# Differential attention: VectorE combines the first half of each tile, GpSimd the rest with a scalar form; transposes two steps behind

## Chip, cores and metric

One Trainium2 chip, one of its cores. The metric is the device time of one execution in microseconds (us): the median of three runs for the kernel before. The engines are TensorE (PE, its weight loads PEld), VectorE (DVE), ScalarE (ACT), GpSimd (POOL) and SyncE (SP), which issues most transfers.

## The reference, cut to what matters

One layer of a hybrid backbone: a projection, differential attention beside a short gated convolution, an output projection. 2048 sample tokens attend to 2048 own and 128 cached keys, with 4 heads of two score maps each; 128 prompt tokens attend to themselves. Everything is float32.

```python
s = einsum('bqhmd,bkhmd->bhmqk', qblk, k) * scale   # m = 0, 1: two maps a head
p = softmax(s, axis=-1)
a = p[:, :, 0] - lam * p[:, :, 1]
out = einsum('bhqk,bkhe->bqhe', a, v)
```

So the map a of a query tile is e0 * c0 + e1 * c1, where e0 and e1 are exponentials of the two maps and c0, c1 factors for each row (reciprocal of the row's sum, for the second map times -lam).

## The kernel before

The program has three stages: modulation, norm and input projections (to about 925 us), attention (about 930 to 1705 us), gated norm and output projection (to the end). The change touches the attention stage alone.

Attention runs over 64 tiles n = 4 * it + t, each 128 queries of one head against 2176 keys. Keys come in PIECES: columns 0 to 1023, 1024 to 2047, and the cached piece 2048 to 2175. Each engine has an order written out by hand: `step(it, t)` with four phases p, in loops over `it` with t unrolled. Phase p of a step makes the scores of map p // 2 and half p % 2 of tile n in one of two pairs of PSUM banks; the cached pieces of both maps share bank 4. Older tiles are worked on in the same step, and the constants S_COMB, S_TR, S_PV and S_OUT say by how many steps they lag.

For one tile:

- TensorE (`scores`, L761) makes the scores; VectorE takes the negated maximum of each 1024 columns (L1380) and of the cached pieces (L1411); ScalarE takes the exponential into e0 (four buffers) and e1 (two buffers) in SBUF, with row sums (L1070, cached pieces L1057). The scores of phase p + 2 need the banks that the exponential of phase p reads.
- VectorE brings the pieces' maxima together (L1402, L1405), ScalarE takes factors (L1082), and in phase 0 of the next step VectorE makes sums and reciprocals (L1388, L1394, L1398).
- GpSimd (`factors`) waits for the reciprocals, makes the row factors (L596, L598), scales the three pieces of e1 (L603) and the middle piece of e0 (L606) and adds the middle piece (L610). Scaling is a tensor_tensor product with the factor repeated along the row.
- VectorE (`combine`, L1362) does the first and the cached piece in one instruction each, two steps later: e0 * c0 + scaled e1. The first stands in phase 0, between the first maximum and the copy of transposes; the cached one in phase 2, before the cached pieces' maxima.
- TensorE (`transposes`, L742) turns the 17 blocks of the map around, three steps behind, in groups of 4, 4, 4, 4 and 1. ScalarE copies groups 0, 1, 2 and 4 to `at` (L1023), VectorE group 3 (`tr_dve`, L1355). Groups 1 and 3 share a bank, so group 1 of the next tile waits for VectorE's copy (t_dve).
- TensorE (`product`, L750) multiplies pairs of tiles with the values, half of the key blocks in each step; ScalarE evacuates (`att_out`, L1031) and stores (`att_store`).

SyncE loads the queries of the next `it` tile by tile behind the scores (L389), the keys of the next head, and the values of a new head in two parts (`load_v`, L402) once the last product on the old ones is done. After tile 63 the steps drain; the prompt's attention and the first output weights are worked in between (`prompt_maps`, `wo_lo`, L1347).

VectorE's phase 0 before, as the order in its queue:

```python
reduce max p0; combine(n - 2, first piece); L1388; tr_dve(n - 4); L1394; L1398
```

Of the kernel before, what the change touches and what calls it, by code (L numbers as in the profile page):

```python
# [26 lines left out]
ALU = mybir.AluOpType  # L27
# [3 lines left out]
P = 128  # L31
# [30 lines left out]
S_COMB, S_TR, S_PV, S_OUT = 2, 3, 5, 7  # L62
# [12 lines left out]
def hymba_layer(nc, a):  # L75
# [8 lines left out]
    with ctx:  # L84
# [25 lines left out]
        tick = sb("tick", [P, 1])  # L110
        cw = sb("cw", [P, 4])
# [199 lines left out]
        def _(sp):  # L311
# [157 lines left out]
            for it in range(ITS):  # L469
                head = it // 4  # L470
                for t in range(4):
# [6 lines left out]
                    if it % 4 == 0 and head > 0 and t == 3:  # L478
                        sp.wait_ge(pv_mm, 4 * it - 1)
                        load_v(head, 0)  # L480
                    if it % 4 == 1 and head > 0 and t == 0:
                        sp.wait_ge(pv_mm, 4 * (it - 1))
                        load_v(head, 1)
# [62 lines left out]
        def _(pool):  # L546
# [46 lines left out]
            def factors(n, t):  # L593
# [7 lines left out]
                for c in (0, 2, 1):  # L601
                    k0, k1 = PIECES[c]
                    pool.tensor_tensor(e1[:, b, k0:k1], e1[:, b, k0:k1],  # L603
                                       stt[:, b, 7, 3 + c:4 + c].to_broadcast([P, k1 - k0]), ALU.mult)\
                        .then_inc(e1_done, 1)
                pool.tensor_tensor(e0[:, t, k0:k1], e0[:, t, k0:k1], stt[:, b, 7, 1:2].to_broadcast([P, k1 - k0]), ALU.mult)\  # L606
                    .then_inc(e0_done, 1)
                pool.wait_ge(e1_done, 3 * (n + 1))
                pool.wait_ge(e0_done, n + 1)
                pool.tensor_tensor(e0[:, t, k0:k1], e0[:, t, k0:k1], e1[:, b, k0:k1], ALU.add).then_inc(a1_ready, 1)  # L610
# [9 lines left out]
        def _(pe):  # L620
# [109 lines left out]
            def transposes(n, t, g):  # L730

                j0, cnt = TGROUPS[g]
                if g == 0:
                    pe.wait_ge(a_ready, 2 * (n + 1))
                    pe.wait_ge(a1_ready, n + 1)
# [28 lines left out]
            def step(it, t, sc=True, tr=True, tr_last=True, pv=True):  # L764
                n = 4 * it + t
                for p in range(4):
# [12 lines left out]
                    if pv:  # L779
                        half = 1 - t % 2  # L780
                        b = 0 if t in (1, 2) else 1
                        if p == 1 - half:
                            pe.wait_ge(s_v[half], (32 if half else 16) * ((it + (2 if t == 0 else 3)) // 4))
                            if half == 0:
                                pe.wait_ge(t_act, 4 * (n - 4) + 3)
                                wait(pe, att_evac, 2 * it - (2 if t == 1 else 1))
                            else:
                                pe.wait_ge(t_act, 4 * (n - 4))
                                pe.wait_ge(t_dve, n - 4)
# [18 lines left out]
            for n in range(NT, NT + S_PV):  # L808
# [3 lines left out]
                if n == NT + 4:  # L812
# [42 lines left out]
        def _(act):  # L855
# [170 lines left out]
            def att_out(it, t):  # L1026

                pb = 1 if t == 1 else 0
                act.wait_ge(pv_mm, 4 * it + t - S_PV)
                wait(act, att_stored[pb], 16 * (it - (2 if t == 1 else 1)))  # L1030
                act.activation(atto[:, pb], ps[:, 7, pb * 2 * P:(pb + 1) * 2 * P], ACT.Copy).then_inc(att_evac, 1)  # L1031

            def att_store(it, t):

                pb = 1 if t == 1 else 0
                act.wait_ge(att_evac, 2 * it - (2 if t == 1 else 1))
                u = it - (2 if t == 1 else 1)
# [7 lines left out]
            def step(it, t, sc=True, tr=True, tr_last=True, out=True):  # L1045
                n = 4 * it + t
                b = t % 2
                for p in range(4):
# [3 lines left out]
                    if sc and p == 3:  # L1052
                        act.wait_ge(mxc_done, n + 1)
                        wait(act, a_ready, 2 * (n - 1))
# [6 lines left out]
                    if sc:  # L1061
# [3 lines left out]
                        if p == 2:  # L1065
                            wait(act, a_ready, 2 * (n - 1) - 1)
                        if p == 3:
                            wait(act, a1_ready, n - 1)
# [15 lines left out]
            for it in range(3):  # L1084
                for t in range(4):
                    n = 4 * it + t
                    step(it, t, tr=n >= S_TR, tr_last=n > S_TR, out=n >= S_OUT and t % 2 == 1)
            with act.Fori(3, ITS) as it:
                for t in range(4):
                    step(it, t, out=t % 2 == 1)  # L1090
            for n in range(NT, NT + S_OUT - 1):
                step(n // 4, n % 4, sc=False, tr=n < NT + S_TR, tr_last=n <= NT + S_TR,
                     out=n % 2 == 1)
# [4 lines left out]
                if n == NT + 2:  # L1098
                    act.wait_ge(a_ready, 2 * NT)
# [46 lines left out]
        def _(dve):  # L1146
# [211 lines left out]
            def combine(n, t, c):  # L1358

                k0, k1 = PIECES[c]  # L1360
                dve.wait_ge(e1_done, 3 * n + (1 if c == 0 else 2))
                dve.scalar_tensor_tensor(e0[:, t, k0:k1], e0[:, t, k0:k1], stt[:, t % 2, 7, c:c + 1],  # L1362
# [8 lines left out]
            def step(it, t, sc=True, den=True, comb=True, tr_last=True):  # L1371
                n = 4 * it + t
                b = t % 2
                for p in range(4):
# [9 lines left out]
                    if p == 0 and comb:  # L1384
                        combine(n - S_COMB, (t - S_COMB) % 4, 0)
# [4 lines left out]
                    if p == 0 and tr_last:  # L1390
# [168 lines left out]
```

## Time and profile before

| | us |
|---|---|
| median of 3 runs (1937.11 to 1943.31) | 1938.04 |
| the profiled execution | 1940.76 |
| its span | 1939.0 |
| TensorE busy | 1763.6 |
| VectorE busy | 1173.9 |
| ScalarE busy | 720.2 |
| GpSimd busy | 749.1 |

The mean granted TensorE clock is 0.971 of full speed. Busy times are sums over the whole span; a matmul's end is modelled, so TensorE's busy time is not work at peak. In lists of groups, a line shows the engine, the operation, output and input, shapes, count, busy time and the mean of one, and behind the bar the idle time in front of it with what ended it. In a timeline, columns are start and length in us; the bracket gives the idle time of the engine just before and its releaser.

### The profile page before, as it was taken

The numbers are of one execution on the slowest core, as the hardware profiler recorded it, in microseconds if no ns is written. First come the engines' busy times: TensorE is split into PE (matmuls) and PEld (weight loads), VectorE is DVE, ScalarE is ACT, GpSimd is POOL, SyncE is SP. The second block draws the span as 40 slices with busy tenths as digits, with TensorE's granted clock in tenths as the row PEclk, the third lists the DMA queues.
The fourth block names the chain that finished last, engine by engine and source line by source line (L and its number), as shares of the span: only waits on it lengthen the run. The fifth ranks groups of instructions, "written<-read, shape, count | busy, mean of one in ns | idle before, by whom it ended". The sixth has DMA issues, their size and how long they took to land.

```text
span 1939.0 us, 25390 instructions
## 1 busy us (share of the span) xinstructions
PE 1763.6 (91%) x8596; PEld 1488.4 (77%) x8596; DVE 1173.9 (61%) x1500; ACT 720.2 (37%) x1505; POOL 749.1 (39%) x614
## 2 busy tenths in 40 slices
PE   7799999989999999998589999889999999659999
PEld 2478888878999989998367777767777777548889
DVE  0554588872232332423688888888888888655553
ACT  2443233331010100100466666666666666431110
POOL 0000488880000000000477777777777777400000
PEclk9899999999999999999799999999999999879999
DMA  9233222331020110101710031113001100146441
GB/s 352 95 109 104 80 99 91 105 117 52 29 90 19 41 68 28 68 19 45 186 35 29 27 85 39 31 47 79 27 27 51 53 27 16 46 170 241 176 141 48
DMA packets 121890, 154.79 MB, mean 80 GB/s; under 512 B 10224, under 2 KB 111344, under 8 KB 120688
## 3 DMA queue, kind: packets, MB, share of 16 engines
q1 hardware_dynamic: 116704, 149.69, 24.0%
q10 hardware_dynamic: 5136, 4.46, 0.7%
q8 instruction: 28, 0.46, 0.1%
q14 instruction: 22, 0.18, 0.0%
HBM read 104.04 MB, written 50.07 MB: 79 GB/s over the span
## 4 chain that ended last, share of the span: by engine, by line
PE 68%; DVE 16%; issue 6%; DMA 4%; ACT 3%; SPq 2%; POOL 0%; DVEq 0%; ACTq 0%; POOLq 0%
PE ps L634 34%; PE ps L836 10%; PE ps L761 8%; DVE e L1362 8%; PE ps L750 7%; PE ps L742 4%; PE ps L626 3%; DVE stt L1380 2%; ACT scr L919 2%; PE ps L651 2%; DVE at L1355 1%; DMA wad<-in_w_ada 1%; PE ps L819 1%; DMA worw<-in_w_out 1%; ACT scr L881 1%
## 5 line engine op out<-in xcount | busy, mean ns | idle before, releaser
L634 PE MATMUL ps<-hT,w 128*128 128x448 f32 (+1 forms) x3360 | 694.1, 366 | 12.6 <-DVE w L1169 12.6
L634 PEld LDWEIGHTS ps<-hT,w 128*128 128x128 f32 x3360 | 623.9, 189 | 76.2 <-issue 27.1
L761 PE MATMUL ps<-kb,qb 128*128 (+1 forms) x1280 | 340.0, 397 | 47.9 <-ACT e L1070 30.8
L1070 ACT ACTIVATE e<-ps,stt 128x1024 f32<-128x1024 f32 x256 | 285.7, 1116 | 259.3 <-DVE stt L1380 235.7
L1380 DVE TENSOR_REDUCE stt<-ps 128x1 f32<-128x1024 f32 x256 | 312.2, 1220 | 97.3 <-PE ps L761 96.9
L750 PE MATMUL ps<-at,vb 128*128 128x256 f32 x1088 | 281.2, 390 | 9.2 <-ACT atto L1031 9.2
L761 PEld LDWEIGHTS ps<-kb,qb 128*128 128x128 f32 x1280 | 208.1, 194 | 84.3 <-ACT e L1070 39.3
L596 POOL TENSOR_TENSOR stt<-stt,lamc 128x2 f32<-128x2 f32 x64 | 12.6, 197 | 660.9 <-DVE stt L1398 660.9
L603 POOL TENSOR_TENSOR e<-e,stt 128x1024 f32<-128x1024 f32 (+1 forms) x192 | 262.8, 1397 | 5.0
L750 PEld LDWEIGHTS ps<-at,vb 128*128 128x128 f32 x1088 | 211.1, 197 | 48.4 <-issue 9.7
L742 PE MATMUL ps<-cst,e 128*128 128x128 f32 x1088 | 175.7, 280 | 57.6 <-DVE at L1355 56.6
L1362 DVE SCALAR_TENSOR_TENSOR e<-e,stt 128x1024 f32<-128x1024 f32 (+1 forms) x128 | 225.6, 1762 | 0.0
L742 PEld LDWEIGHTS ps<-cst,e 128*128 128x128 f32 x1088 | 131.0, 142 | 112.0 <-DVE at L1355 82.1
L836 PE MATMUL ps<-mix,wo 128*128 128x448 f32 (+1 forms) x960 | 205.1, 373 | 7.2 <-DVE mix L1455 7.2
L836 PEld LDWEIGHTS ps<-mix,wo 128*128 128x128 f32 x960 | 181.7, 192 | 27.5 <-DVE mix L1455 7.6
L610 POOL TENSOR_TENSOR e<-e 128x1024 f32<-128x1024 f32 x64 | 152.5, 2383 | 9.2
L985 ACT ACTIVATE scr<-ps 128x448 f32<-128x448 f32 (+1 forms) x40 | 20.9, 533 | 352.7 <-PE ps L634 352.7
L1217 DVE RECIPROCAL qx<-qx 128x448 f32<-128x448 f32 (+1 forms) x40 | 114.8, 2870 | 49.8 <-ACT qx L950 49.7
L565 POOL TENSOR_TENSOR qx<-qx,scr 128x448 f32<-128x448 f32 (+1 forms) x40 | 45.8, 1146 | 241.3 <-DVE qx L1221 238.9
L1023 ACT ACTIVATE at<-ps 128x512 f32<-128x512 f32 (+1 forms) x256 | 124.3, 511 | 23.1 <-PE ps L742 22.8
L606 POOL TENSOR_TENSOR e<-e,stt 128x1024 f32<-128x1024 f32 x64 | 125.2, 1956 | 0.0
L634 PE MATMUL ps<-w,hT 128*128 128x512 f32 x408 | 98.1, 401 | 7.3 <-DVE hT L1201 7.3
(108 smaller groups left out, 1374.4 us busy)
## 6 DMA issues: line engine op xcount, KB each, us to landing
raw<-in_w_in SPq DMA_DIRECT2D x32, 512.0 KB, 3.8
qb<-spill_q SPq DMA_DIRECT2D x256, 64.0 KB, 2.3
wad<-in_w_ada SPq DMA_DIRECT2D x6, 2048.0 KB, 9.0
scr<-in_xT SPq DMA_DIRECT2D x8, 1024.0 KB, 5.7
kb<-spill_k SPq DMA_DIRECT2D x8, 1024.0 KB, 9.7
spill_k<-scr SPq DMA_DIRECT2D x32, 224.0 KB, 2.1
spill_q<-scr SPq DMA_DIRECT2D x32, 224.0 KB, 2.2
spill_cv<-scr SPq DMA_DIRECT2D x32, 224.0 KB, 2.2
```

What stands on the lines that cost most here:

```text
L603: pool.tensor_tensor(e1[:, b, k0:k1], e1[:, b, k0:k1], stt[:, b, 7, 3 + c:4 + c].to_broadcast([P, k1 - k0]), ALU.mult)\
L606: pool.tensor_tensor(e0[:, t, k0:k1], e0[:, t, k0:k1], stt[:, b, 7, 1:2].to_broadcast([P, k1 - k0]), ALU.mult)\
L610: pool.tensor_tensor(e0[:, t, k0:k1], e0[:, t, k0:k1], e1[:, b, k0:k1], ALU.add).then_inc(a1_ready, 1)
L634: mm = pe.matmul(out, slot_of(l, j), rhs_of(r, j), start=(i == 0 and j == 0), stop=(i == 2 and j == DJ - 1))
L742: mm = pe.transpose(trbank(g)[:, i * P:(i + 1) * P], e0[:, t, (j0 + i) * P:(j0 + i + 1) * P], ident)
L750: mm = pe.matmul(ps[:, 7, b * 2 * P:(b + 1) * 2 * P], vb[:, js[i]], at[:, b, 0, js[i], :], start=(half == 0 and i == 0), stop=(half == 1 a ...
L761: mm = pe.matmul(out[:, c0 - k0:c1 - k0], qb[:, t, ver, m], keys, start=(ver == 0), stop=(ver == 1))
L836: mm = pe.matmul(ps[:, k % 4, 0:n], wo[:, o, l, j], mix[:, tg % 2, r, j, 0:n], start=(half == 0 and i == 0 and j == H), stop=(half == 1 an ...
L1023: act.activation(at[:, t // 2, 0, j0:j0 + cnt, (t % 2) * P:(t % 2 + 1) * P], trbank(g).rearrange("p (j q) -> p j q", j=cnt), ACT.Copy).the ...
L1070: act.activation(dst[:, c * 1024:(c + 1) * 1024], ps[:, 2 * c:2 * c + 2, :].rearrange("p c n -> p (c n)"), ACT.Exp, bias=stt[:, b, 0, 3 * ...
L1362: dve.scalar_tensor_tensor(e0[:, t, k0:k1], e0[:, t, k0:k1], stt[:, t % 2, 7, c:c + 1], e1[:, t % 2, k0:k1], ALU.mult, ALU.add).then_inc(a ...
L1380: dve.tensor_reduce(stt[:, b, 0, 3 * m + c:3 * m + c + 1], ps[:, 2 * c:2 * c + 2, :].rearrange("p c n -> p (c n)"), AX.X, ALU.max, negate= ...
```

## The change

- VectorE keeps one combine a tile, of the first piece. It is issued one step behind the scores (two before), in phase 2 behind the cached pieces' maxima. The copy of transposes moves to directly behind the first maximum.
- GpSimd scales e1 in the order of its pieces and both later pieces of e0, with tensor_scalar and a factor for each partition in place of tensor_tensor, and adds both pieces in one instruction of 1152 columns. A small product into a new tile `gate` stands ahead of the scaling.
- Transposes lag by two steps (three before), products by four (five), the evacuation by six (seven). Group 0 waits for VectorE's combine alone, group 2 for GpSimd's add. All waits on counters, the parity of halves and buffers, and the places of the value loads are moved to match. The drain has one step less.

```diff
-S_COMB, S_TR, S_PV, S_OUT = 2, 3, 5, 7
+S_COMB, S_TR, S_PV, S_OUT = 1, 2, 4, 6
...
+        gate = sb("gate", [P, 2])
...
-                    if it % 4 == 0 and head > 0 and t == 3:
+                    if it % 4 == 0 and head > 0 and t == 2:
...
-                    if it % 4 == 1 and head > 0 and t == 0:
-                        sp.wait_ge(pv_mm, 4 * (it - 1))
+                    if it % 4 == 0 and head > 0 and t == 3:
+                        sp.wait_ge(pv_mm, 4 * it)
...
-                for c in (0, 2, 1):
+                pool.tensor_tensor(gate[:], lamc[:], lamc[:], ALU.mult)
+                for c in range(3):
...
-                    pool.tensor_tensor(e1[:, b, k0:k1], e1[:, b, k0:k1],
-                                       stt[:, b, 7, 3 + c:4 + c].to_broadcast([P, k1 - k0]), ALU.mult)\
+                    pool.tensor_scalar(e1[:, b, k0:k1], e1[:, b, k0:k1], stt[:, b, 7, 3 + c:4 + c], None, ALU.mult)\
...
-                pool.tensor_tensor(e0[:, t, k0:k1], e0[:, t, k0:k1], stt[:, b, 7, 1:2].to_broadcast([P, k1 - k0]), ALU.mult)\
-                    .then_inc(e0_done, 1)
+                for c in (1, 2):
+                    k0, k1 = PIECES[c]
+                    pool.tensor_scalar(e0[:, t, k0:k1], e0[:, t, k0:k1], stt[:, b, 7, c:c + 1], None, ALU.mult)\
+                        .then_inc(e0_done, 1)
...
-                pool.wait_ge(e0_done, n + 1)
-                pool.tensor_tensor(e0[:, t, k0:k1], e0[:, t, k0:k1], e1[:, b, k0:k1], ALU.add).then_inc(a1_ready, 1)
+                pool.wait_ge(e0_done, 2 * (n + 1))
+                pool.tensor_tensor(e0[:, t, 1024:KEYS], e0[:, t, 1024:KEYS], e1[:, b, 1024:KEYS], ALU.add)\
+                    .then_inc(a1_ready, 1)
...
-                    pe.wait_ge(a_ready, 2 * (n + 1))
+                    pe.wait_ge(a_ready, n + 1)
+                if g == 2:
                    pe.wait_ge(a1_ready, n + 1)
...
-                        half = 1 - t % 2
-                        b = 0 if t in (1, 2) else 1
+                        half = t % 2
+                        b = t // 2
...
-                            pe.wait_ge(s_v[half], (32 if half else 16) * ((it + (2 if t == 0 else 3)) // 4))
+                            pe.wait_ge(s_v[half], (32 if half else 16) * ((it + 3) // 4))
...
-                                pe.wait_ge(t_act, 4 * (n - 4) + 3)
-                                wait(pe, att_evac, 2 * it - (2 if t == 1 else 1))
+                                pe.wait_ge(t_act, 4 * (n - 3) + 3)
+                                wait(pe, att_evac, 2 * it - (2 if t == 0 else 1))
...
-                                pe.wait_ge(t_act, 4 * (n - 4))
-                                pe.wait_ge(t_dve, n - 4)
+                                pe.wait_ge(t_act, 4 * (n - 3))
+                                pe.wait_ge(t_dve, n - 3)
...
-                if n == NT + 4:
+                if n == NT + 3:
...
             def att_out(it, t):
...
-                pb = 1 if t == 1 else 0
+                pb = 1 if t == 0 else 0
...
-                wait(act, att_stored[pb], 16 * (it - (2 if t == 1 else 1)))
+                wait(act, att_stored[pb], 16 * (it - (2 if t == 0 else 1)))
...
             def att_store(it, t):
...
-                pb = 1 if t == 1 else 0
-                act.wait_ge(att_evac, 2 * it - (2 if t == 1 else 1))
-                u = it - (2 if t == 1 else 1)
+                pb = 1 if t == 0 else 0
+                act.wait_ge(att_evac, 2 * it - (2 if t == 0 else 1))
+                u = it - (2 if t == 0 else 1)
...
-                        wait(act, a_ready, 2 * (n - 1))
+                        wait(act, a1_ready, n - 1)
...
-                            wait(act, a_ready, 2 * (n - 1) - 1)
-                        if p == 3:
-                            wait(act, a1_ready, n - 1)
+                            wait(act, a_ready, n - 1)
...
-                    step(it, t, tr=n >= S_TR, tr_last=n > S_TR, out=n >= S_OUT and t % 2 == 1)
+                    step(it, t, tr=n >= S_TR, tr_last=n > S_TR, out=n >= S_OUT and t % 2 == 0)
...
-                    step(it, t, out=t % 2 == 1)
+                    step(it, t, out=t % 2 == 0)
...
-                     out=n % 2 == 1)
+                     out=n % 2 == 0)
...
-                    act.wait_ge(a_ready, 2 * NT)
+                    act.wait_ge(a_ready, NT)
...
-            def combine(n, t, c):
...
-                k0, k1 = PIECES[c]
-                dve.wait_ge(e1_done, 3 * n + (1 if c == 0 else 2))
-                dve.scalar_tensor_tensor(e0[:, t, k0:k1], e0[:, t, k0:k1], stt[:, t % 2, 7, c:c + 1],
+            def combine(n, t):
...
+                k0, k1 = PIECES[0]
+                dve.wait_ge(e1_done, 3 * n + 1)
+                dve.scalar_tensor_tensor(e0[:, t, k0:k1], e0[:, t, k0:k1], stt[:, t % 2, 7, 0:1],
...
             def bc(x):
...
-                    if p == 0 and comb:
-                        combine(n - S_COMB, (t - S_COMB) % 4, 0)
+                    if p == 0 and tr_last:
+                        tr_dve(n - 1 - S_TR, (t - 1 - S_TR) % 4)
...
-                    if p == 0 and tr_last:
-                        tr_dve(n - 1 - S_TR, (t - 1 - S_TR) % 4)
...
-                    if p == 2 and comb:
-                        combine(n - S_COMB, (t - S_COMB) % 4, 2)
...
+                    if p == 2 and comb:
+                        combine(n - S_COMB, (t - S_COMB) % 4)
...
-            for n in range(NT, NT + S_TR + 1):
+            for n in range(NT, NT + S_TR + 2):
...
```

## Rows read from the trace of the kernel before

**Rows 1.** The page, part 1: busy time, share of the span and instructions of each engine.

```profile
PE 1763.6 (91%) x8596; PEld 1488.4 (77%) x8596; DVE 1173.9 (61%) x1500; ACT 720.2 (37%) x1505; POOL 749.1 (39%) x614
```

**Rows 2.** Busy time by windows in the attention stage: stretch, its length, engines, granted clock, DMA.

```profile
982.00:1660.00 678.00, 607.64 (x3167) 492.60 (x3168) 578.53 (x764) 441.00 (x1027) 515.42 (x413) 0.98 0.15 40
```

**Rows 3.** Waits from 982 to 1660 us: total, times, longest.

```profile
ACT e L1070 <- DVE stt L1380: 188.4, 219, 2.5
POOL stt L596 <- DVE stt L1398: 145.0, 59, 4.1
...
PE ps L742 <- DVE at L1355: 50.8, 30, 1.7
...
PE ps L761 <- ACT e L1070: 19.2, 30, 0.8
```

**Rows 4.** Timeline of one tile and of the context maximum two tiles on.

```profile
1187.83 0.41 DVE L1411 TENSOR_REDUCE stt<-ps 128x2 f32<-128x256 f32 x1
...
1189.41 1.11 ACT L1070 ACTIVATE e<-ps,stt 128x1024 f32<-128x1024 f32 x1 [0.32 <-DVE stt L1380]
...
1189.81 2.38 POOL L610 TENSOR_TENSOR e<-e 128x1024 f32<-128x1024 f32 x1
1189.85 1.22 DVE L1380 TENSOR_REDUCE stt<-ps 128x1 f32<-128x1024 f32 x1
...
1190.66 1.20 PE L761 MATMUL ps<-kb,qb 128*128 x4 [0.69 <-ACT e L1070]
1190.99 2.27 DVE L1362 SCALAR_TENSOR_TENSOR e<-e,stt 128x1024 f32<-128x1024 f32 x1
1191.19 1.11 ACT L1070 ACTIVATE e<-ps,stt 128x1024 f32<-128x1024 f32 x1 [0.21 <-DVE stt L1380]
...
1193.26 0.68 DVE L1355 COPY at<-ps 128x512 f32<-128x512 f32 x1
...
1194.00 0.66 PE L742 MATMUL ps<-cst,e 128*128 128x128 f32 x4 [1.70 <-DVE at L1355]
...
1194.29 0.20 POOL L596 TENSOR_TENSOR stt<-stt,lamc 128x2 f32<-128x2 f32 x1 [2.10 <-DVE stt L1398]
...
1194.84 4.10 POOL L603 TENSOR_TENSOR e<-e,stt 128x1024 f32<-128x1024 f32 x3
...
1198.90 1.94 POOL L606 TENSOR_TENSOR e<-e,stt 128x1024 f32<-128x1024 f32 x1
...
1210.52 0.41 DVE L1411 TENSOR_REDUCE stt<-ps 128x2 f32<-128x256 f32 x1
```

**Rows 5.** Groups by shape, 930 to 1690 us.

```profile
L1380 DVE TENSOR_REDUCE stt<-ps 128x1 f32<-128x1024 f32 x256 | 312.2, 1220 | 97.3 <-PE ps L761 96.9
...
L1362 DVE SCALAR_TENSOR_TENSOR e<-e,stt 128x1024 f32<-128x1024 f32 x64 | 116.2, 1815 | 0.0
...
L1362 DVE SCALAR_TENSOR_TENSOR e<-e,stt 128x128 f32<-128x128 f32 x64 | 109.4, 1709 | 0.0
```

**Rows 6.** Timeline of the drain.

```profile
1666.14 0.33 DVE L1362 SCALAR_TENSOR_TENSOR e<-e,stt 128x128 f32<-128x128 f32 x1
...
1670.95 2.87 POOL L606 TENSOR_TENSOR e<-e,stt 128x1024 f32<-128x1024 f32 x1
...
1681.98 1.28 DVE L1362 SCALAR_TENSOR_TENSOR e<-e,stt 128x1024 f32<-128x1024 f32 x1
...
1683.91 1.11 PE L742 MATMUL ps<-cst,e 128*128 128x128 f32 x4 [3.92 <-DVE at L1355]
```

**Rows 7.** Timeline of TensorE's weight loads, a quarter of a step: its first and its end.

```profile
1185.87 0.76 PEld L761 LDWEIGHTS ps<-kb,qb 128*128 128x128 f32 x4
...
1188.10 0.77 PEld L761 LDWEIGHTS ps<-kb,qb 128*128 128x128 f32 x4
```

**Rows 8.** Timeline near the start of attention: L1405.

```profile
947.19 1.30 DVE L1405 TENSOR_TENSOR stt<-stt 128x6 f32<-128x6 f32 x1
```

**Rows 9.** DMA issues: count, KB each, median us from issue to landing.

```profile
vb<-spill_v SPq DMA_DIRECT2D x4, 576.0 KB, 4.0
```

## Prediction

> **What bounds the kernel now.** The page's busy shares come first [rows 1]: TensorE 91%, no other engine above 61%. That is a mean over stages; the change lies only in the attention stage, 64 query tiles from about 930 to 1700 us, so I read that one. The windows [rows 2] give for 982 to 1660 us TensorE 607.6 of 678 us, 90%, so 70 us of idle time in 59 tiles (GpSimd waits for reciprocals 59 times, once a tile [rows 3]), 1.2 us each. VectorE is busy 578.5 and GpSimd 515.4 us there: both are close behind. The waits [rows 3] name what TensorE's idle time ends with: 50.8 us on VectorE's copy of transposes (L1355), 19.2 us on ScalarE's exponential (L1070). The exponential itself waits for VectorE's maxima (188.4 us).
>
> The timeline of one tile [rows 4] shows why. GpSimd's add starts at 1189.81 and lasts 2.38 us. VectorE starts its 1024-column combine at 1190.99; it lasts 2.27 us and ends 1.07 us behind the end of the add. Behind it in VectorE's queue stands the copy (1193.26), and TensorE's next transposes start at 1194.00 after 1.70 us of idle time. The 128-column combine is worse by its size: 1709 ns on average [rows 5], 0.33 us when GpSimd is idle [rows 6]. So a VectorE instruction with two inputs in SBUF stands still until GpSimd's current instruction ends. It works the other way too: beside VectorE's L1347, GpSimd's L606 takes 2.87 us at 1670.95 [rows 6] in place of 1.94 at 1198.90 [rows 4].
>
> A tile takes (1210.52 - 1187.83) / 2 = 11.35 us by the context maxima of tiles two apart [rows 4]; over the 678 us it is 11.49, since the granted clock is 0.98 of 2.4 GHz on average there [rows 2]. I take that as unchanged.
>
> **The parts and their cost, for a tile.**
> *TensorE: nothing added.* A quarter of a step (4 score matmuls, 4 product instructions, 4 transposes) runs from 1185.87 to 1188.10, 2.23 us [rows 7]. Four are 8.9; the context scores (4 shorter matmuls, which I estimate at half of the quarter's 4 long ones, 0.45), the 17th transpose (0.14) and the odd product instruction (0.21) make 9.7 to 9.9 us. I take 9.85: the floor, 1.5 us below today.
>
> *VectorE.* It loses the 128-column combine (0.33 us of work, 1.71 with its wait), keeps the 1024-column one (1.28 us when alone [rows 6], 1815 ns on average [rows 5]), and the copy now stands directly behind the first maximum. Work: 4 maxima of 1.22, context 0.41, combine 1.28, copy 0.68 and five small ones of some 0.16, 8.0 us. That is under the floor; only its waits count. The wait of the transposes for the copy falls from 1.70 us to about 0.2 in even tiles: first maximum 1.2 us after its scores, copy done 1.8 later, the transposes due at 2.8.
>
> *GpSimd.* Small operations 0.55 us (1194.29 to 1194.84 [rows 4]) and one more, the gate, some 0.27: 0.82. Scaling grows from 3200 columns to 2176 + 1152 = 3328. The add grows to 1152 columns, 2.38 x 1.125, with its gap 2.8. The combine holds GpSimd up once, 1.1. At today's price for scaling, 4.10 for 2176 columns [rows 4] and 1.94 + 0.3 for 1152, the total is 0.82 + 6.35 + 2.8 + 1.1 = 11.1 us. **The unknown is the price of the scalar form**, which no row shows. Upper end: the same as L603, (4.10 - 0.3) / 2 = 1.90 for 1024 columns. Lower end: 1.22, the price of the one-stream maximum on VectorE (L1380) [rows 5]; another engine, so a far row. Two full streams cost 2.38 (L610) [rows 4] and one stream with a repeated scalar 1.90; I take the same step of 0.48 once more, 1.42. That saves 3.25 x 0.48 = 1.56: a loop of 9.5 us. To it comes up to 0.6 us (from VectorE's small operations to GpSimd's first) where GpSimd has to wait for the reciprocals: 10.1. At the lower end it is 8.9.
> The Trainium skill, GPSIMD Engine Reference, section Engine selection, says that one-input operations on GpSimd run at about line rate and two-input ones about twice as slowly. By it the scaling would be near my lower end, and the sum the one of the first rival; no run here shows it yet.
>
> *The combine's new place.* It stands between the context maxima and the last maximum, and GpSimd is in mid-stream there. VectorE's next instruction starts some 0.08 us before the end of the one ahead (1189.85 + 1.22 against 1190.99) [rows 4], so the maximum takes 1.14, the context 0.33, the combine 1.20, and the last maximum starts 2.66 us behind the third, where TensorE spaces the scores by 2.23: 0.4 late. The wait for the end of a scaling is half of 1.42 on average, 0.7. From the last maximum to the scores of the next tile that need its bank it is 2.6 us (maximum to exponential 1.34, 1189.85 to 1191.19; exponential to score 1.25, 1189.41 to 1190.66), and 1.2 from the last scores to an undelayed maximum: 3.8 together. TensorE gets there 3.8 us behind the last scores where little product work lies between, every second tile, and 5.5 in the others. So every second tile loses all of 0.4 + 0.7 = 1.1, the others nothing: 0.55 per tile. With 0.1 for the copy and 0.1 for L1405, another two-input instruction (1.30 us when it met GpSimd [rows 8], one of the small ones otherwise), the tile takes 9.85 + 0.75 = 10.6 us.
>
> *Transposes two steps behind.* ScalarE's first exponential no longer waits for the last transposes of the same step; what that gives is inside the 1.5 us already. The transposes of tile n need the combine of the step before, ready 1.5 us early, and GpSimd's add only for their third group, some 4 us early. Behind that new wait stand the third transposes and the last scores; if GpSimd is later than that, it is the bound, below. The value loads get fewer steps: each issue waits for the last product on the old values, and lands 4.0 us later [rows 9], with more than a step (10 us) until its first product; the query load queued behind it on SP is for the next iteration, 40 us away. Cost 0. The buffers' waits in ScalarE (second tensor of exponentials) now name work finished a step earlier: 0.
>
> *Drain.* After the last tile VectorE works off the prompt's maps before the copy that TensorE waits for (3.92 us, 1683.91 [rows 6]), unchanged. Behind it lies one step less: some 3.7 us of product and 2.4 of transposes, part of which an output-weight load may eat. I take 5 (0 to 7).
>
> **Sum.** 11.35 - 10.6 = 0.75 x 62 steady tiles = 46.5, plus 5: 51.5 us off. The profiled execution took 1940.8 us (span 1939.0), 2.7 above the median of 1938.0. 1940.8 - 51.5 - 2.7 = **1886.5 us**. Own range: 10.4 to 10.8 us a tile, 1874 to 1901.
>
> **Rivals.**
> *TensorE becomes the bound.* The scalar form costs 1.2 or less, GpSimd is done early and VectorE meets it rarely: 10.1 to 10.3 us, 1.15 x 62 = 71 + 6: 1861. For it: the one-input form. Against: three two-input VectorE instructions per tile still meet GpSimd.
> *The port takes it back.* The combine or L1405 falls into the 2.7 us add instead of a 1.4 us scaling. Every second tile then loses 2.7 rather than 1.1, and the next maximum is late too: about 11.1 us, 0.25 x 62 + 4 = 20 off: 1918. For it: L1362 waits in both its forms today [rows 5], and the add is GpSimd's longest instruction. Against: where the combine sits, a scaling is due, not the add. The Trainium skill, SBUF — State Buffer, section Who interferes with whom, states the block as a rule: a VectorE instruction with two SBUF inputs against a GpSimd one that reads SBUF, and the second to come stands still until the other ends. By that rule, which the trace bears out, moving the combine into mid-stream speaks against the change.
> *GpSimd becomes the bound, slower than before.* The scalar form costs what L603 costs. The loop is 11.1 with reciprocals ready in time (16 off, and up to 5 in the drain: 1917 to 1922; nearer to no change with some of the latency), and 11.7 where the add ends first and reciprocals come after it: +0.35 x 62 - 5 = +17: 1955 from the median of 1938. It decides from a scaling price of about 1.8 us per 1024 columns, where the loop with its latency passes 11.35. For it: the loop scales 4% more columns and adds 12.5% more. Against: an operand less.
> *The change does nothing*: waits only change names; 1938.
>
> **Chances.** Forecast 0.42; TensorE bound 0.18; port 0.15; GpSimd bound without the latency 0.08 (0.05 of it faster by more than 0.3%); nothing 0.05; slower 0.12. 0.3% is 5.8 us, about what a measurement can tell here. Faster 0.42 + 0.18 + 0.15 + 0.05 = 0.80, the same 0.08, slower 0.12. The range goes from the TensorE bound (1856) to just short of no change (1936): below lies little, above the slower case and part of no change.
>
> **What would show it.** Right: GpSimd's TENSOR_SCALAR near 1.4 us, the context maxima 10.6 us apart, TensorE's wait for L1355 nearly gone, its wait for L1070 up, combine about 1.9 us on average, VectorE's idle time larger. Wrong: scalings at 1.9 us and GpSimd's idle time before L596 (145.0 us now [rows 3]) gone; or combines over 3 us beside the add; or a new TensorE wait for GpSimd's add before the third group of transposes.

## The result, and the profile after

The changed kernel takes 2032.2 us (median of 4, 2030.65 to 2033.11) against 1937.6 before: ratio 1.048, 95% interval 1.046 to 1.050. It is slower by 94.6 us, where 51.5 us less were forecast, outside the stated range. Experiment 6 below had one slow execution, of 3503 us; its time is given as 1906.0 us, the median of its other three, where the recorded expectations name 1906.9, the median of all four.

The groups of the attention stage in the profile after (by shape, 930 to 1790 us) name the cause in their first line:

```profile
L605 POOL TENSOR_SCALAR e<-e,stt 128x1024 f32<-128x1024 f32 x128 | 362.6, 2845 | 0.1
...
L609 POOL TENSOR_SCALAR e<-e,stt 128x1024 f32<-128x1024 f32 x64 | 182.0, 2844 | 0.0
L613 POOL TENSOR_TENSOR e<-e 128x1152 f32<-128x1152 f32 x64 | 169.3, 2646 | 5.6
...
L1365 DVE SCALAR_TENSOR_TENSOR e<-e,stt 128x1024 f32<-128x1024 f32 x64 | 136.4, 2131 | 136.7 <-POOL e L605 136.7
...
L605 POOL TENSOR_SCALAR e<-e,stt 128x128 f32<-128x128 f32 x64 | 40.0, 625 | 0.0
```

Before, the same view (930 to 1690 us) had these two lines for e1:

```profile
L603 POOL TENSOR_TENSOR e<-e,stt 128x1024 f32<-128x1024 f32 x128 | 242.5, 1895 | 5.0
...
L603 POOL TENSOR_TENSOR e<-e,stt 128x128 f32<-128x128 f32 x64 | 25.7, 402 | 0.0
```

A scaling of 1024 columns in the scalar form takes 2.845 us, where the tensor_tensor form with a repeated factor took 1.895. The operation with fewer operands is half as dear again. VectorE was idle for 136.7 us in front of its combine (L1365), waiting for the first scaling of e1 (L605).

The timeline of GpSimd over one tile after, with what stands beside it (start, length):

```profile
1188.37 0.20 POOL L597 TENSOR_TENSOR stt<-stt,lamc 128x2 f32<-128x2 f32 x1
...
1189.09 6.25 POOL L605 TENSOR_SCALAR e<-e,stt 128x1024 f32<-128x1024 f32 x3
...
1191.97 2.13 DVE L1365 SCALAR_TENSOR_TENSOR e<-e,stt 128x1024 f32<-128x1024 f32 x1 [1.69 <-POOL e L605]
...
1195.32 3.42 POOL L609 TENSOR_SCALAR e<-e,stt 128x1024 f32<-128x1024 f32 x2
...
1195.54 0.90 DVE L1406 TENSOR_TENSOR stt<-stt 128x6 f32<-128x6 f32 x1
...
1198.83 2.65 POOL L613 TENSOR_TENSOR e<-e 128x1152 f32<-128x1152 f32 x1
...
1201.43 0.19 POOL L597 TENSOR_TENSOR stt<-stt,lamc 128x2 f32<-128x2 f32 x1
...
1207.22 0.66 PE L747 MATMUL ps<-cst,e 128*128 128x128 f32 x4 [1.69 <-DVE e L1365]
```

L597 opens each tile's work on GpSimd, and none of its rows here has idle time in front of it: from 1188.37 to 1201.43 it works without a gap, 13.06 us. Before, L596 had waited 2.10 us there [rows 4]. The loop is 0.72 of small operations, 6.23 for e1, 3.51 for e0 and 2.60 for the add. The other engines wait for it in turn, TensorE at L747 through the combine. The windows from 982 to 1740 us say the same: GpSimd busy 744 of 758 us, TensorE 646 (85%, before 90% [rows 2]), and a granted clock of 0.91:

```profile
982.00:1740.00 758.00, 646.12 (x3138) 523.58 (x3137) 533.68 (x697) 436.15 (x1016) 744.01 (x523) 0.91 0.14 36
```

A tile took 11.52 us before and takes 13.06 now (means over 40 tiles, between the 6th and the 46th context maximum from 980 us on; all tile times below are made so). 1.54 x 62 = 95 us: the loss lies in the tiles. The stall that the change was to remove did go: TensorE's wait for the copy, 50.8 us before [rows 3], is no longer among its larger waits after. A wait of the same size, for the combine, has taken its place (982 to 1740 us):

```profile
PE ps L766 <- ACT e L1073: 58.5, 47, 1.7
PE ps L747 <- DVE e L1365: 50.8, 29, 1.9
```

### The profile page after: what moved, and what is told of

It is laid out like the page before. It is cut to its first block, busy times and chain, and to the rows that moved or that the text cites. A ratio compares the mean times of both kernels' runs of the same rounds, so it can differ in the third digit from the quotient of the medians.

```text
span 2028.9 us, 25262 instructions
## 1 busy us (share of the span) xinstructions
PE 1809.1 (89%) x8596; PEld 1528.5 (75%) x8596; DVE 1133.4 (56%) x1436; ACT 720.6 (36%) x1505; POOL 1007.0 (50%) x742
## 4 chain that ended last, share of the span: by engine, by line
PE 47%; POOL 31%; issue 12%; DVE 4%; DMA 3%; ACT 3%; SPq 0%; POOLq 0%; ACTq 0%; DVEq 0%
PE ps L638 33%; POOL e L605 19%; PE ps L841 9%; POOL e L613 6%; POOL e L609 3%; PE ps L630 3%; ACT scr L924 2%; PE ps L655 1%; DMA wad<-in_w_ada 1%; PE ps L824 1%; POOL stt L599 1%; DMA worw<-in_w_out 1%; POOL gate L602 1%; ACT scr L886 1%; DVE crs L1444 1%
## 5 line engine op out<-in xcount | busy, mean ns | idle before, releaser
L766 PE MATMUL ps<-kb,qb 128*128 (+1 forms) x1280 | 371.0, 426 | 87.2 <-ACT e L1073 68.7
L605 POOL TENSOR_SCALAR e<-e,stt 128x1024 f32<-128x1024 f32 (+1 forms) x192 | 401.1, 2105 | 0.1
L766 PEld LDWEIGHTS ps<-kb,qb 128*128 128x128 f32 x1280 | 231.2, 216 | 134.8 <-issue 54.9
L755 PE MATMUL ps<-at,vb 128*128 128x256 f32 x1088 | 285.9, 394 | 0.0
L597 POOL TENSOR_TENSOR stt<-stt,lamc 128x2 f32<-128x2 f32 x64 | 12.6, 196 | 504.9 <-DVE stt L1399 504.9
L747 PE MATMUL ps<-cst,e 128*128 128x128 f32 x1088 | 188.7, 293 | 63.8 <-DVE e L1365 54.4
L747 PEld LDWEIGHTS ps<-cst,e 128*128 128x128 f32 x1088 | 143.8, 151 | 115.8 <-issue 36.2
L609 POOL TENSOR_SCALAR e<-e,stt 128x1024 f32<-128x1024 f32 (+1 forms) x128 | 219.2, 1725 | 0.0
L1365 DVE SCALAR_TENSOR_TENSOR e<-e,stt 128x1024 f32<-128x1024 f32 x64 | 136.4, 2131 | 136.7 <-POOL e L605 136.7
L613 POOL TENSOR_TENSOR e<-e 128x1152 f32<-128x1152 f32 x64 | 169.3, 2646 | 5.6
```

The costliest lines, as they stand in the source:

```text
L605: pool.tensor_scalar(e1[:, b, k0:k1], e1[:, b, k0:k1], stt[:, b, 7, 3 + c:4 + c], None, ALU.mult)\
L609: pool.tensor_scalar(e0[:, t, k0:k1], e0[:, t, k0:k1], stt[:, b, 7, c:c + 1], None, ALU.mult)\
L613: pool.tensor_tensor(e0[:, t, 1024:KEYS], e0[:, t, 1024:KEYS], e1[:, b, 1024:KEYS], ALU.add)\
L747: mm = pe.transpose(trbank(g)[:, i * P:(i + 1) * P], e0[:, t, (j0 + i) * P:(j0 + i + 1) * P], ident)
L755: mm = pe.matmul(ps[:, 7, b * 2 * P:(b + 1) * 2 * P], vb[:, js[i]], at[:, b, 0, js[i], :], start=(half == 0 and i == 0), stop=(half == 1 a ...
L766: mm = pe.matmul(out[:, c0 - k0:c1 - k0], qb[:, t, ver, m], keys, start=(ver == 0), stop=(ver == 1))
```

## The experiments

Each is timed against the kernel before on the same chip. The chips are four: experiments 1 to 3 ran on one, 5 to 8 on another, 9 to 11 on a third, 12 and 13 on a fourth, and the kernel before took 1938.5, 1940.7, 1938.7 and 1938.5 us on them. Differences of a few us between experiments of different chips are therefore uncertain by some 2 us.

| | us | ratio to before, 95% | us per tile |
|---|---|---|---|
| 1 changed, tensor_tensor form | 1917.3 | 0.988 (0.984 to 0.991) | 11.22 |
| 2 before, scalar form | 2022.6 | 1.042 (1.039 to 1.045) | 13.03 |
| 3 changed, constant factor (one execution) | 2004.1 | | 12.62 |
| 4 changed, scaling and add in one instruction | no result | | |
| 5 as 1, no gate | 1906.4 | 0.983 (0.981 to 0.985) | 11.08 |
| 6 as 5, one scaling on ScalarE | 1906.0 | 0.981 (0.979 to 0.983) | 11.08 |
| 7 changed, one scaling on ScalarE | 1893.1 | 0.976 (0.975 to 0.978) | 10.85 |
| 8 as 1, lags of before | 1923.7 | 0.992 (0.990 to 0.993) | 11.22 |
| 9 as 6, factors' differences on ScalarE | 1860.8 | 0.960 (0.958 to 0.962) | 10.29 |
| 10 as 7, the same | 1864.9 | 0.960 (0.958 to 0.963) | 10.30 |
| 11 as 5, the same | 1906.2 | 0.983 (0.981 to 0.986) | 11.08 |
| 12 before, with both additions of 9 | 1891.1 | 0.976 (0.973 to 0.979) | 10.74 |
| 13 changed, differences on ScalarE | 2033.6 | 1.049 (1.046 to 1.052) | 13.07 |

**1. The changed kernel with the old form.**

```diff
-pool.tensor_scalar(e1[:, b, k0:k1], e1[:, b, k0:k1], stt[:, b, 7, 3 + c:4 + c], None, ALU.mult)
+pool.tensor_tensor(e1[:, b, k0:k1], e1[:, b, k0:k1], stt[:, b, 7, 3 + c:4 + c].to_broadcast([P, k1 - k0]), ALU.mult)
...
-pool.tensor_scalar(e0[:, t, k0:k1], e0[:, t, k0:k1], stt[:, b, 7, c:c + 1], None, ALU.mult)
+pool.tensor_tensor(e0[:, t, k0:k1], e0[:, t, k0:k1], stt[:, b, 7, c:c + 1].to_broadcast([P, k1 - k0]), ALU.mult)
```

> The changed kernel, with GpSimd's five scalings back in the tensor_tensor form with a repeated factor (columns, order, gate, lags and all waits as changed). Theory P (price of the scalar form): scalings fall from 2.84 to 1.9 us per 1024 columns, GpSimd's loop from 13.06 to 10.1 us plus up to 1.1 for VectorE's combine; a tile takes 10.8 to 11.3 us and the kernel 1890 to 1920 us, faster than before. Theory S (the schedule: the combine in mid-stream on VectorE and the shorter lag of the transposes cost the time): it stays above 1980 us whatever the scalings cost.

Measured: 1917.3 us. Theory P holds: 115 us lie in the form alone, and the rest of the change, the gate included, is worth 21 us of gain. The timeline of this kernel:

```profile
1179.06 5.08 POOL L605 TENSOR_TENSOR e<-e,stt 128x1024 f32<-128x1024 f32 x3
...
1180.99 2.90 DVE L1365 SCALAR_TENSOR_TENSOR e<-e,stt 128x1024 f32<-128x1024 f32 x1
...
1185.32 0.69 DVE L1406 TENSOR_TENSOR stt<-stt 128x6 f32<-128x6 f32 x1
...
1187.67 1.43 DVE L1391 TENSOR_TENSOR stt<-stt 128x6 f32<-128x6 f32 x1
...
1189.58 0.20 POOL L597 TENSOR_TENSOR stt<-stt,lamc 128x2 f32<-128x2 f32 x1 [0.49 <-DVE stt L1399]
...
1200.80 0.20 POOL L597 TENSOR_TENSOR stt<-stt,lamc 128x2 f32<-128x2 f32 x1 [0.49 <-DVE stt L1399]
```

The combine starts at 1180.99, just behind the start of the second scaling, and ends at 1183.89: it takes 1.6 us longer than alone (1.28 us [rows 6]) and then holds GpSimd up itself (the three scalings of e1 take 5.08 here, 4.10 before [rows 4]). The three two-input instructions of VectorE (L1365, L1406, L1391) take 5.0 us in a tile, against 1.28 + 0.17 + 0.15 alone: 3.4 us of waiting. GpSimd idles 0.49 us for the reciprocals.

**2. The kernel before with the new form**, and the gate.

```diff
+pool.tensor_tensor(gate[:], lamc[:], lamc[:], ALU.mult)
-pool.tensor_tensor(e1[:, b, k0:k1], e1[:, b, k0:k1], stt[:, b, 7, 3 + c:4 + c].to_broadcast([P, k1 - k0]), ALU.mult)
+pool.tensor_scalar(e1[:, b, k0:k1], e1[:, b, k0:k1], stt[:, b, 7, 3 + c:4 + c], None, ALU.mult)
...
-pool.tensor_tensor(e0[:, t, k0:k1], e0[:, t, k0:k1], stt[:, b, 7, 1:2].to_broadcast([P, k1 - k0]), ALU.mult)
+pool.tensor_scalar(e0[:, t, k0:k1], e0[:, t, k0:k1], stt[:, b, 7, 1:2], None, ALU.mult)
```

> The kernel before, with its scalings on GpSimd in the tensor_scalar form and the gate ahead of them, nothing else. Theory P: GpSimd's loop is 0.8 of small ones + 2 x 2.84 + 0.6 + 2.84 + 0.1 + 2.4 = 12.4 us and becomes the bound, with the latency of the reciprocals up to 13.0; the kernel takes 2000 to 2045 us, so that the form alone makes it as slow as the whole change. Theory S: GpSimd's waiting time of 2.5 us per tile hides most of it and it stays within 1940 to 1965 us.

Measured: 2022.6 us, 13.03 us a tile. The form, with the gate, costs 84 us in the old schedule. With the first experiment it brackets the cause from both sides. The gate stands in this kernel and in the changed one; from start to start it takes 0.28 us, so that its part where GpSimd has no gap is 0.28 x 62 = 17 us by an estimate. No run takes it out of a kernel with the scalar form.

**3. A constant in place of the factor.** The row factors are left out of the scaled pieces here.

```diff
-pool.tensor_scalar(e1[:, b, k0:k1], e1[:, b, k0:k1], stt[:, b, 7, 3 + c:4 + c], None, ALU.mult)
+pool.tensor_scalar(e1[:, b, k0:k1], e1[:, b, k0:k1], 0.25, None, ALU.mult)
...
-pool.tensor_scalar(e0[:, t, k0:k1], e0[:, t, k0:k1], stt[:, b, 7, c:c + 1], None, ALU.mult)
+pool.tensor_scalar(e0[:, t, k0:k1], e0[:, t, k0:k1], 0.25, None, ALU.mult)
```

> The changed kernel, with the constant 0.25 in place of the factor read from SBUF in all five scalings (the row factors are left out of the scaled pieces, so the maps lack their reciprocals there). If reading the factor per partition is what makes the form slow, a scaling of 1024 columns falls well below 1.9 us and the kernel below 1930. If the form itself is slow, it stays at 2.84 us and the kernel at 2032.

The groups of this kernel:

```profile
L605 POOL TENSOR_SCALAR e<-e 128x1024 f32<-128x1024 f32 x128 | 352.4, 2771 | 0.0
...
L605 POOL TENSOR_SCALAR e<-e 128x128 f32<-128x128 f32 x64 | 34.2, 535 | 0.0
```

Measured: 2004.1 us in one execution, 12.62 us a tile. Reading the factor costs 0.07 us, the form 2.77. It is the form. The kernel is 28 us faster than the 2032 expected, since each of the five scalings is 0.07 to 0.09 us shorter: 0.4 us a tile. The difference between 1024 and 128 columns is 2.24 us for 896, 2.5 ns a column, so it is a cost of each column and not of starting. For the tensor_tensor form the same working gives (1895 - 402) / 896 = 1.7 ns a column.

**4. GpSimd's scaling and add of e0 in one instruction** (scalar_tensor_tensor), with e1 scaled in the tensor_tensor form. It was expected to take 1860 to 1890 us if the fused form cost what the add does, and 1880 to 1920 us if forms with a factor for each partition are slow as a family. There is no result, so the price of that form on GpSimd, and whether such forms are slow as a family, stay open.

**5. Without the gate.** One instruction of 0.19 us (0.28 from start to start) less on GpSimd.

```diff
-pool.tensor_tensor(gate[:], lamc[:], lamc[:], ALU.mult)
```

> The first experiment (tensor_tensor form in the changed schedule) without the small gate operation. There GpSimd's loop is 11.22 us and nearly closed (L597 at 1189.58 and 1200.80), so theory P, in which that loop sets the tile, wants 0.27 us less per tile: 10.9 to 11.0 us and 1897 to 1908 us. If VectorE's chain (busy 640 of 658 us, waits included) or TensorE sets the pace, the gate is hidden and the time stays at 1917.

Measured: 1906.4 us; a tile 0.14 shorter, so that 11.08 us is just above the 10.9 to 11.0 expected. Some 9 to 11 us for one tiny instruction: GpSimd's loop is on the path also with the cheap form, but about half of what is taken from it comes back in waits. The change's schedule alone, with the old form and no gate, is worth 34 us of gain (1906.4 against 1940.7 on that chip).

**6. One scaling moved to ScalarE** (tensor_tensor form). GpSimd scales e1's cached piece first here, then the middle one.

```diff
+if fac and p == 1:
+    act.wait_ge(coef_done, n)
+    act.activation(e1[:, 1 - b, 0:1024], e1[:, 1 - b, 0:1024], ACT.Copy, scale=stt[:, 1 - b, 7, 3:4]).then_inc(sc_done, 1)
...
-for c in range(3):
+for c in (2, 1):
...
-dve.wait_ge(e1_done, 3 * n + 1)
+dve.wait_ge(sc_done, n + 1)
```

> The changed schedule with the tensor_tensor form and no gate, and the scaling of e1's first piece moved from GpSimd to ScalarE (one copy of 1024 columns with a factor per partition, in phase 1). GpSimd's loop loses 1.9 us: 11.0 - 1.9 = 9.1. Theory P: GpSimd is off the critical path, TensorE's 9.85 us and the waits of the maxima are left, a tile takes 10.1 to 10.6 us and the kernel 1845 to 1885 us. If meeting GpSimd at the port is the dearer part, VectorE's waits keep the tile at 10.8 or more, above 1895 us.

Measured: 1906.0 us, 11.08 us a tile: the same as without the move. Theory P missed; its rival, a tile of 10.8 us or more and over 1895 us, came true. GpSimd now waits 2.30 us before L598, in the first line (982 to 1660 us), so it is not the bound. The timeline shows what is:

```profile
POOL stt L598 <- DVE stt L1403: 136.8, 60, 2.3
```

```profile
1191.51 2.63 POOL L613 TENSOR_TENSOR e<-e 128x1152 f32<-128x1152 f32 x1
...
1192.35 0.16 DVE L1407 TENSOR_REDUCE stt<-stt 128x2 f32<-128x6 f32 x1
...
1192.55 1.61 DVE L1410 TENSOR_TENSOR stt<-stt 128x6 f32<-128x6 f32 x1
...
1194.08 1.21 DVE L1387 TENSOR_REDUCE stt<-ps 128x1 f32<-128x1024 f32 x1
1194.19 0.21 ACT L1089 ACTIVATE stt<-stt 128x6 f32<-128x6 f32 x1 [0.71 <-DVE stt L1410]
```

A subtraction of 6 columns takes 1.61 us in place of 0.17: it has two inputs in SBUF, arrives in the middle of the add and ends with it (1194.16 against 1194.14). The reduction just ahead of it (L1407), with one input in SBUF, takes 0.16 us beside the same add. The next tile's first maximum and ScalarE's factors stand behind the subtraction. This is the rival of the prediction in which L1405 is caught by the add.

**7. The same move with the slow form kept** (gate too).

> The same move to ScalarE, with GpSimd's other four scalings kept in the changed kernel's tensor_scalar form and the gate kept. GpSimd's loop is 13.06 - 2.84 = 10.2 us. Theory P: the tile takes 10.2 to 10.8 us and the kernel 1855 to 1900 us, though the form is slow. VectorE's combine meets the scalar form for 0.85 us (2.13 against 1.28) where it stood 1.6 us beside the other form (2.87), so it may come close to the version with the tensor_tensor form. If the scalar form harms in another way than by its length, it stays above 1930 us.

Measured: 1893.1 us, 12.9 less than with the fast form. The expectation held for the kernel's time, and its second half more than I had thought; the tile, 10.85 us, is just above the 10.2 to 10.8. The groups of this kernel:

```profile
L610 POOL TENSOR_SCALAR e<-e,stt 128x1024 f32<-128x1024 f32 x64 | 204.7, 3198 | 0.0
...
L614 POOL TENSOR_TENSOR e<-e 128x1152 f32<-128x1152 f32 x64 | 169.6, 2649 | 9.5
...
L1370 DVE SCALAR_TENSOR_TENSOR e<-e,stt 128x1024 f32<-128x1024 f32 x64 | 98.7, 1542 | 47.6 <-ACT e L1086 47.6
...
L1411 DVE TENSOR_TENSOR stt<-stt 128x6 f32<-128x6 f32 x64 | 19.0, 297 | 2.2
```

and of the sixth, VectorE's two:

```profile
L1369 DVE SCALAR_TENSOR_TENSOR e<-e,stt 128x1024 f32<-128x1024 f32 x64 | 120.2, 1879 | 13.5 <-ACT e L1085 10.8
L1410 DVE TENSOR_TENSOR stt<-stt 128x6 f32<-128x6 f32 x64 | 102.4, 1600 | 2.2
```

Here the combine takes 1.54 us on average and the subtraction 0.30, against 1.88 and 1.60 in the sixth. GpSimd is fuller, but VectorE waits less at it.

**8. The lags of the kernel before**, in the first experiment's kernel.

```diff
-S_COMB, S_TR, S_PV, S_OUT = 1, 2, 4, 6
+S_COMB, S_TR, S_PV, S_OUT = 1, 3, 5, 7
```

with the parities, counters and load places of before.

> The first experiment with the lags of the kernel before: transposes three steps behind, products five, the evacuation seven, with their parities and load places; the new split of the work and VectorE's new order are kept. Theory P: the shorter lag is worth only the drain, so 1917 plus 3 to 8 us. Theory S would have the shorter lag cost time in every tile: then it is faster than 1917 by 10 us or more.

Measured: 1923.7 us with the same 11.22 us a tile. Transposes two steps behind are worth some 4 to 6 us: 6.4 between the two medians, 4.2 when each is set against the kernel before on its own chip. They lie in the drain: from the last context maximum to the end of the program it is 281.5 us here and 275.9 in experiment 1.

**9 to 11. The subtraction taken from VectorE**, in the sixth, seventh and fifth kernels. ScalarE forms the differences inside the exponentials, two of 0.29 us in place of one of 0.21.

```diff
-act.wait_ge(d_done, n + 1)
-act.activation(stt[:, b, 3, :], stt[:, b, 2, :], ACT.Exp).then_inc(f_done, 1)
+act.wait_ge(gm_done, n + 1)
+for m in range(2):
+    fm = act.activation(stt[:, b, 3, 3 * m:3 * m + 3], stt[:, b, 0, 3 * m:3 * m + 3], ACT.Exp,
+                        scale=-1.0, bias=stt[:, b, 5, 2 + m:3 + m])
+fm.then_inc(f_done, 1)
...
-dve.tensor_tensor(three(stt[:, b, 2, :]), bc(stt[:, b, 5, 2:4]), three(stt[:, b, 0, :]), ALU.subtract)
```

> The sixth experiment (tensor_tensor form, e1's first piece scaled on ScalarE; 1906.9 us, a tile 11.07 us) with VectorE's small two-input subtraction taken away: ScalarE takes the differences inside its two exponentials of the factors. Theory Q (the port holds the tile: the subtraction stands 1.43 us behind GpSimd's 2.6-us add in every tile, and the factors, the next maximum and the copy stand behind it): a tile loses 0.5 to 1.0 us, 10.1 to 10.6 us, the kernel 1845 to 1880. Rival R (ScalarE, 76% busy there, or TensorE sets the pace): at most 10 us off, above 1895.

> The seventh experiment (tensor_scalar form, e1's first piece on ScalarE; 1893.1 us) with the same subtraction taken away. There it waited only 0.13 us on average (297 ns for one), and the product L1396 waits 0.83 us behind the add instead. Theory Q: 0 to 0.3 us per tile, 1875 to 1893, a far smaller gain than in its neighbour, since the wait it removes is small. Rival R: the same small change in both.

> The fifth experiment (tensor_tensor form, no gate, all scalings on GpSimd; 1906.4 us, a tile 11.09 us) with the same subtraction taken away. GpSimd's loop there is closed but for 0.5 us (10.6 busy with the combine's hold-up). Theory P: GpSimd stays the bound, so the removal of a VectorE wait gives at most 0.5 us per tile, 1875 to 1906. If VectorE's chain set the tile instead, it would gain the 0.5 us of wait and more, below 1870.

The ninth took 1860.8 us and 10.29 us a tile, inside theory Q's ranges: some 45 us from one instruction of 6 columns, 0.79 us in each tile. The windows of it, 982 to 1600 us:

```profile
982.00:1600.00 618.00, 595.41 (x3247) 500.80 (x3245) 475.90 (x655) 511.45 (x1160) 508.97 (x420) 1.00 0.17 46
```

TensorE is busy 96% here: it is the bound at last. The tenth gained 28.2 us, more than the 0 to 18 expected, a miss: the VectorE product ahead of the reciprocals (L1396 in the seventh, L1399 here) falls from 984 to 303 ns on average too, so moving one instruction took the next one out of the add's way. The eleventh gained nothing (1906.2): all scalings are on GpSimd there, its loop of 11.08 us is closed but for 0.5, and the wait saved at the subtraction reappears at the product (1884 ns on average). So the same edit is worth 45, 28 or 0 us, depending on who sets the tile.

**12. Both additions without the change.**

> The kernel before (its schedule, split and lags) with the two additions of the ninth experiment: ScalarE scales e1's first piece and takes the factors' differences. GpSimd's loop shrinks to 7.2 us, which it had 2.5 us to spare for anyway; VectorE's combines still stand ahead of the copy, but the add ahead of them ends about 1.9 us earlier. If the additions alone make the ninth fast, this comes within 10 us of 1861. If the changed kernel's order on VectorE and its lags carry part of it, as I hold, this lands at 1880 to 1930 us.

Measured: 1891.1 us, within the band for the changed kernel's schedule carrying a part. The additions alone bring 47 us, and the change's own schedule 30.3 on top of them, the ninth's time being 1860.8. The other order of counting agrees: the schedule first is worth 34 us (experiment 5) and the additions then some 44 to 46. The schedule is the new split of the work, VectorE's order and the lags together; only the lags were tried by themselves (experiment 8).

**13. The changed kernel without the subtraction's wait.**

> The changed kernel with the factors' differences on ScalarE and nothing else: the 0.73-us wait of VectorE's subtraction in every tile goes, GpSimd's loop of 13.06 us stays. Theory P: GpSimd alone sets the tile, so the kernel stays within 5 us of 2032. If VectorE's waits at the port are part of what made the change slow, it gains 0.3 to 0.7 us per tile, 1985 to 2012.

Measured: 2033.6 us, no change. VectorE's waits at the port cost nothing in the changed kernel, since GpSimd alone sets its tile.

## Why the prediction was wrong, step by step

- **The price of the scalar form: the step that failed.** "Upper end: the same as L603" took for granted that an operand less can't cost more, and the chosen 1.42 carried a trend on from two rows. It measured 2.84. In the loop this term is 3.25 x 1.42 = 4.6 us larger than taken. The prediction's loop of 9.5 us becomes 14.1 by it; 13.06 was measured (0.72 + 9.74 for the five scalings + 2.60), since the hold-up of 1.1 in that sum did not occur. Experiments 1 and 2 put 115 and 84 us on the form, the second with the gate. By the Trainium skill, GPSIMD Engine Reference, section Engine selection, one-input operations run at about line rate and two-input ones about twice as slowly; for this form the runs say the opposite (2.84 us for one input, 2.38 for the add with two [rows 4]), and the measurement decides.
- **GpSimd becomes the bound.** The mechanism was among the rivals, with 0.12 where slower, but its price ended at L603's, so 1955 was the worst that it gave. It would have decided "from a scaling price of about 1.8 us". At 1.89 (experiment 1) the kernel was still faster: the loop came to 10.73 of work and hold-up plus 0.49 for the reciprocals, 11.22, near the 11.1 given and under the 11.7 that I feared. The 1917 to 1922 stated for that case met 1917.3, in part by luck: the loop's work was 0.4 us less than the 11.1 taken with reciprocals in time, and the wait for them gave it back. The sign of being wrong came as stated, but for the price: GpSimd's idle time before its first instruction of a tile (145.0 us before [rows 3]) is gone.
- **The combine's new place.** The hold-up of GpSimd, taken as 1.1, measured 0.97 with the old form (the 128-column scaling behind the combine takes 1.38 in place of 0.41) and 0 with the new. Its wait, taken as 0.7 on average, was 1.6 with the old form and 0.85 with the new. The 0.7 took the meeting for one at a random moment of a scaling. It is not random: the combine needs e1's first piece, so it can't start before the first scaling ends. In the timelines it starts 0.06 us (changed kernel) and 0.08 us (experiment 1) behind the start of the second scaling, and meets that one from its beginning.
- **L1405 at 0.1 us: mis-sized.** It waits 0.73 us in the changed kernel and 1.43 in experiment 6, where it sets the tile; taking it away gave 45 us. The port rival had the mechanism right.
- **The copy.** Right: the wait of 50.8 us went. The new wait of 50.8 us for the combine is GpSimd's lateness.
- **TensorE's floor.** 9.85 us was the estimate, and 10.1 to 10.3 the tile with TensorE as the bound, 1861 us. Experiment 9 reached 10.29 us and 1860.8 with TensorE 96% busy, which is 9.9 us a tile and agrees with the floor. It is another kernel than the rival's, so that the same microsecond is luck.
- **The tile before.** The sum starts from 11.35 us, one pair of tiles; the mean is 11.52. From there to the 10.6 forecast it would have been 57 us and not 46.5. It doesn't bear on the direction.
- **The lags and the drain.** Taken as 5 us, measured 4 to 6 (experiment 8); nothing in a tile, as said. In the changed kernel the gain doesn't show: from the last context maximum to the end it is 278.6 us, and 279.1 before.
- **SP's loads: 0.** No wait for values or queries is among the larger ones after.

## What to carry to other kernels

An operation whose price no row shows has no upper end in the row of a richer operation: on GpSimd the form with fewer operands was the dearer one here (2.84 us against 1.90). Run the one instruction before a schedule is built on it. An engine with 2 us to spare in 11 turned into the bound when three long scalings on it changed their form (experiment 2), and what is won elsewhere is then invisible (experiment 13). A tiny VectorE instruction with two inputs in SBUF can cost what is left of a long GpSimd one that it meets (1.43 us for 6 columns); on ScalarE the same work made one exponential of 0.21 us into two of 0.29.

## What the runs showed that I had not expected

GpSimd's two forms keep VectorE waiting in different ways. In the old form a scaling holds a two-input VectorE instruction off until it ends: the combine takes 2.90 us at 1180.99. In the changed kernel the combine at 1191.97 stands beside this scaling, the second of the merged row of L605:

```profile
1191.92 2.85 POOL L605 TENSOR_SCALAR e<-e,stt 128x1024 f32<-128x1024 f32 x1
```

It starts 0.06 us behind it and takes 2.13, so that it ends 0.7 us ahead of that scaling's end, and the subtraction at 1195.54 ends 1.12 us behind the start of its scaling. In experiment 1 a held combine ends 1.08 us behind the end of what held it, and a held product (L1391) 0.02. Taken off here, both leave 1.1 us. So both fit a shared port that comes free for VectorE some 1.1 us into the instruction, while GpSimd works on for 1.7 more; no experiment tried that by itself. With the combine first it is the other way round, and the scaling grows to 3.2 us on average (L610, experiment 7). The Trainium skill, SBUF — State Buffer, section Who interferes with whom, has the port held for the whole instruction; the old form agrees, the new one doesn't. This fits experiment 7 being faster than 6: its subtraction stands deep in a long scaling and takes 0.30 us, where in experiment 6 GpSimd is already at its add and holds it for 1.43. Without the subtraction on VectorE the advantage is gone (1864.9 us with the slow form, 1860.8 with the fast one). What GpSimd does in the remaining time stays open.

The granted clock fell behind a stretch in which TensorE was mostly idle. In windows of 2 us of the changed kernel TensorE is busy 0.65 and 0.43 of 2.00 us at 1180 and 1182. Then the clock is 0.64 of 2.4 GHz, a window with both levels in it, and 0.51, the 1.2 GHz level, before it is back at 1.00:

```profile
1180.00:1182.00 2.00, 0.65 (x4) 0.42 (x4) 2.00 (x2) 0.00 (x0) 2.00 (x2) 1.00 0.76 236
1182.00:1184.00 2.00, 0.43 (x2) 0.44 (x3) 1.85 (x4) 1.49 (x4) 2.00 (x2) 1.00 0.14 40
1184.00:1186.00 2.00, 2.00 (x9) 1.52 (x8) 1.93 (x6) 1.67 (x5) 1.92 (x3) 0.64 0.00 0
1186.00:1188.00 2.00, 2.00 (x9) 1.77 (x8) 0.76 (x1) 1.70 (x5) 2.00 (x1) 0.51 0.19 66
1188.00:1190.00 2.00, 2.00 (x10) 1.71 (x10) 1.27 (x2) 0.49 (x2) 1.84 (x5) 1.00 0.00 0
```

The mean is 0.91 in the changed kernel's stage and 1.00 in experiment 9's. The lower clock is a consequence here: GpSimd's loop of 13.06 us sets the tile at either clock.
